# Expert outputs kept as rows in device memory and fetched by each token, for seven of eight experts

## The chip, the cores and the metric

The kernel runs on one core of one Trainium2 chip. The metric is the device time of one execution in microseconds (us); three runs of the kernel before give 1876.14 us as their median.

## The reference, cut to what matters

Two layers of a hybrid decoder trunk (four mixer groups, cross attention, a feed-forward part) on 256 tokens of 1024 numbers, all in float32. The second layer ends with eight SwiGLU experts, of which each token uses two:

```python
def moe_swiglu(h, router, wg, wu, wd):
    logits = (h @ router).astype(jnp.float32)
    top_v, top_i = lax.top_k(logits, TOP_K)                 # TOP_K = 2
    gates = jax.nn.softmax(top_v, axis=-1)
    combine = jnp.sum(jax.nn.one_hot(top_i, N_EXPERTS, dtype=jnp.float32) * gates[..., None], axis=-2)
    out = jnp.zeros_like(h)
    for e in range(N_EXPERTS):                              # 8 experts, wg and wu 1024x3584, wd 3584x1024
        out = out + combine[..., e:e + 1].astype(h.dtype) * swiglu(h, wg[e], wu[e], wd[e])
    return out
```

## The kernel before

The first 880 us are the two layers up to the experts. The change touches only `experts()`, of which every engine has its own copy (ACT L858, DVE L1500, PE L2323), the block of GpSimd (L1738) and the loads of SP.

**Passes and steps.** An expert is one pass `p` of at most 128 tokens (an expert with more gets a second pass behind the eight; with these inputs none does). A pass has 7 steps `j` of 512 columns of the 3584, so there are 56 steps `s = 7p + j`. Each step uses six chunks of 1 MB of weights: four for gate and up, two for down. SP loads chunk `m` into one of six raw buffers (`ex_raw`, `XRAW = 6`: three of their own, two in `PT`, one in `TMP`) as soon as DVE has read chunk `m - 6` there. ACT copies a chunk to a rounded "hi" (L863), DVE subtracts to get a "lo" (L1023, `x_chunk`), both into one of four pairs of buffers (`XSPL = 4`), which come free when PE has used chunk `m - 4`. PE makes each product in three passes (hi by hi, lo by hi, hi by lo).

**The order of PE** is written out by hand: `turn(s-1)` (four transposes, L2407), `gate_up(s)` (48 matmuls of 512 columns, L2371), `down(s-1)` (24 matmuls, L2381), so the down product of a step comes one step late and hides the activation on ACT and DVE (`prod`, `act_hi`, `act_lo`).

**Tokens to slots.** `one_hots` (DVE, L1551) writes a matrix `oneh` of tokens by slots. `turn_slots(p)` (PE) turns it with two transposes (L2448) and, for `p > 0`, makes the list of token rows with four small matmuls (L2451, two in the source, each as two in the trace). DVE's `turned(p)` takes both out: `slot_index` (L1564) and the turned one-hot `onehT` (L1565). GpSimd fetches the 128 token rows of a pass from `token_rows` in device memory into `picked` with an indirect DMA (L1750), and PE turns them (`gather`, L2462).

**Slots back to tokens.** When pass `q` is done, ACT copies its output to `yE` hi (`expert_output`, L892), DVE makes `yE` lo (`output_lo`, L1558), PE multiplies both with `onehT` (`scatter(q, hf)`, L2480: four matmuls of 512 columns per half, eight per expert), and DVE adds the result, times the gate, into the residual `x` (`scattered`, L1579, four per expert). For the first seven experts the two halves of `scatter` stand before and after `down` in step 1 of the next pass; for the last one they stand at the end.

**Gates and tables.** At `s == 2` DVE runs `gates_and_passes` between the lo of chunk 13 and `act_lo(1)`: 15 small operations in a row. Chunks 14 and 15 are those of `down(1)`.

Of the kernel before, what the change touches and what calls it, by code (L numbers as in the profile page):

```python
# [14 lines left out]
P = 128  # L15
D = 1024
# [93 lines left out]
def build(nc, A, out):  # L110
# [14 lines left out]
    with ExitStack() as ctx:  # L125
# [30 lines left out]
        onehT_flat = shared("onehT", 512, 4 * 1024 * (7 - 4), F32R)  # L156
# [182 lines left out]
        STORED = 16 * (TT + 2)  # L339
        SECONDS = TT * P * 2 // (P + 1)  # L340
        oneh = mt(3)[:, 0:256]
        onehT = [onehT_flat[:, 256 * i:256 * i + 256] for i in range(2)]
# [144 lines left out]
        def _(act):  # L487
# [370 lines left out]
            def experts():  # L858
# [22 lines left out]
                def expert_output(q):  # L881

                    if q == NE - 1:
                        act.wait_ge(S("tm_half"), 6)
                    else:
                        act.wait_ge(S("chunk_done"), n_straight + xd(q * XSTEPS + XSTEPS - 1, 1) + 1)
                    if q:
                        act.wait_ge(S("ex_sc"), 4 * q)
                    for hf in range(2):
                        if hf and q == NE - 1:  # L890
                            act.wait_ge(S("chunk_done"), n_straight + NX)
                        nc.scalar.activation(yE[0][:, 512 * hf:512 * hf + 512], ps[:, 4 + hf, :], ACT.Copy).then_inc(S("ex_yhi"), 1)  # L892
# [43 lines left out]
                added[0] = act.value_load(pass_count[0:1, 0:1], min_val=4 * NE - 1, max_val=4 * (NE + SECONDS) - 1)  # L936
# [60 lines left out]
        def _(dve):  # L997
# [502 lines left out]
            def experts():  # L1500
# [72 lines left out]

                def scattered(q, hf):

                    for t in range(TT):
                        dve.wait_ge(S("ex_sc"), q * 4 + (2 * hf + t + 1))
# [14 lines left out]
                turned(0)  # L1592
# [4 lines left out]
                def gates_and_passes():  # L1597

                    dve.wait_ge(S("rt_p"), 1)
                    for t in range(TT):  # L1600
                        ts(o[:, t, 0, :], o[:, t, 0, :], weight[:, t, 0:1], ALU.mult)
                        stt(gate[:, t, :], o[:, t, 1, :], weight[:, t, 1:2], o[:, t, 0, :], ALU.mult, ALU.add)
# [7 lines left out]
                    ts(col(ST_N1), col(ST_N1), 4.0, ALU.mult, float(4 * NE - 1), ALU.add)  # L1610
# [9 lines left out]
                for s in range(XS):  # L1620
# [17 lines left out]
                    if j == 1 and p:  # L1638
                        scattered(p - 1, 0)
# [4 lines left out]
                    if j == 1 and p:  # L1644
                        scattered(p - 1, 1)
# [14 lines left out]
                for hf in range(2):  # L1660
                    output_lo(hf, 2 * NE - 1 + hf)
                for hf in range(2):
                    scattered(NE - 1, hf)
                for o in range(SECONDS):
                    with dve.If(which[o] < NE):
# [11 lines left out]
                        dve.wait_ge(S("ex_gt"), o + (NE + 1))  # L1677
# [19 lines left out]
                        for hf in range(2):  # L1697
                            for t in range(TT):
                                dve.wait_ge(S("ex_sc"), o * 4 + (4 * NE + 2 * hf + t + 1))
# [38 lines left out]
        def _(pool):  # L1738
            G = nc.gpsimd
            pool.wait_ge(S("eps_xs"), 1 + TT)  # L1740
            for hf in range(2):
                pool.dma_start(token_rows[0:1, 512 * hf:512 * hf + 512], tmp(4)[0:1, :]).then_inc(S("ex_rows"), 16)
# [3 lines left out]
            for p in range(1, NE):  # L1746
                pool.wait_ge(S("ex_index"), p)
                if p > 1:
                    pool.wait_ge(S("ex_g"), 2 * p)
                G.indirect_dma_start(picked, None, token_rows, bass.IndirectOffsetOnAxis(slot_index, 0)).then_inc(S("ex_rows"), 16)  # L1750

        @block.tensor
        def _(pe):
# [569 lines left out]
            def experts():  # L2323
# [118 lines left out]
                def turn_slots(p):  # L2442

                    pe.wait_ge(S("ex_sel"), p * 2 + 2)
                    if p:
                        pe.wait_ge(S("ex_selT"), p)
                    for t in range(TT):
                        ins = pe.transpose(ps[:, 3, P * t:P * t + P], oneh[:, P * t:P * t + P], ident)  # L2448
                    if p:
                        for t in range(TT):  # L2450
                            ins = pe.matmul(ps[:, 3, 256:257], oneh[:, P * t:P * t + P], slot_row[t], start=t == 0, stop=t == 1)  # L2451
                    ins.then_inc(S("ex_gt"), 1)

                def gather(p):

                    if p > 1:
                        pe.wait_ge(S("ex_x"), 4 * (p - 1))
                    if p:
                        pe.wait_ge(S("ex_rows"), STORED + 16 * p)
# [10 lines left out]
                def scatter(q, hf):  # L2470

                    pe.wait_ge(S("ex_y"), q * 2 + (hf + 1))
                    if hf == 0:
                        pe.wait_ge(S("ex_selT"), q + 1)
                        pe.wait_ge(S("ex_hlo"), KT * min(q + 2, NE))
                    for t in range(TT):
                        if hf and q < NE - 1:
                            pe.wait_ge(S("ex_x"), q * 4 + (t + 1))
                        for i in range(2):
                            ins = pe.matmul(ps[:, out_bank(q, hf) + t, :], onehT[q % 2][:, P * t:P * t + P], yE[i][:, 512 * hf:512 * hf + 512],  # L2480
# [6 lines left out]
                turn_slots(0)  # L2487
                for s in range(XS):
# [20 lines left out]
                with pe.Fori(0, SECONDS) as o:  # L2509
                    which = pe.value_load(pass_expert[0:1, bass.ds(o + NE, 1)], min_val=0, max_val=NE)  # L2510
                    with pe.If(which < NE):
# [5 lines left out]
                        pe.wait_ge(S("ex_x"), 4 * NE)  # L2517
# [22 lines left out]
                        pe.wait_ge(S("ex_selT"), o + (NE + 1))  # L2540
                        for hf in range(2):
                            pe.wait_ge(S("ex_y"), o * 2 + (2 * NE + hf + 1))
                            for t in range(TT):
                                if hf:
                                    pe.wait_ge(S("ex_x"), o * 4 + (4 * NE + t + 1))
# [103 lines left out]
```

## Time and profile before

| | |
|---|---|
| median of 3 runs | 1876.14 us (1874.97 to 1878.23) |
| the profiled execution, its own time | 1873.28 us |
| its span, first to last instruction | 1871.4 us (1.9 us lie around it) |
| mean granted TensorE clock | 0.995 |
| busy over the span | PE 97%, weight loads 84%, DVE 76%, ACT 62%, GpSimd 9.1 us |
| moved by DMA | 470.75 MB, mean 252 GB/s; 363 to 395 GB/s while the experts run |

The chain of work that ended last is 92% PE. A busy PE does not mean PE at its peak, since matmuls overlap; what a matmul costs is read from the distance of its start to the next one's, not from its duration. Times in rows are microseconds from the start of the span, means of one are in nanoseconds.

### The profile page before, as it was taken

Reading aid. Unit: us, or ns where it says so; the run is one execution under the profiler, and the core shown is the slowest. Engines: PE = TensorE matmul, PEld = TensorE weight load, DVE = VectorE, ACT = ScalarE, POOL = GpSimd, SP = SyncE. Lnnn points to the kernel's source line nnn. Section 1 sums busy time; section 2 is a strip of 40 time slices with the busy share of each in tenths; the row PEclk is TensorE's granted clock in tenths of the full one; section 3 lists DMA queues with packets and bytes.
Section 4 is the critical chain, followed back from the end, with each engine's and each line's share of the span. In section 5 each row is a group of like instructions: output and inputs, shape, how many; then the busy total and the mean of one; then the engine's idle time right before and its main releaser. Section 6 shows DMA issues by size and latency. Waiting matters only on the chain.

```text
span 1871.4 us, 29948 instructions
## 1 busy us (share of the span) xinstructions
PE 1815.1 (97%) x12628; PEld 1565.2 (84%) x12629; DVE 1429.3 (76%) x1468; ACT 1154.5 (62%) x1127; POOL 9.1 (0%) x15
## 2 busy tenths in 40 slices
PE   7989999999999998999999999999999999999996
PEld 7977789999999977798888888888888888888885
DVE  7875654544458776554999999899998998989986
ACT  6565344443444655445777777777777777767774
POOL 0000000000000000000000000000000000000000
PEclk9999999999999999999999999999999999999998
DMA  8511224455636212235999999999999999999992
GB/s 254 180 59 58 70 91 173 140 191 188 203 127 208 94 48 69 91 136 196 332 380 383 363 366 374 375 374 363 356 381 370 369 368 363 379 371 363 368 374 114
DMA packets 240830, 470.75 MB, mean 252 GB/s; under 512 B 12080, under 2 KB 87984, under 8 KB 240688
## 3 DMA queue, kind: packets, MB, share of 16 engines
q1 hardware_dynamic: 239184, 463.93, 69.1%
q0 software_dynamic: 1360, 4.72, 0.6%
q8 instruction: 102, 1.67, 0.4%
q14 instruction: 40, 0.33, 0.1%
q10 hardware_dynamic: 144, 0.11, 0.0%
HBM read 466.62 MB, written 2.10 MB: 250 GB/s over the span
## 4 chain that ended last, share of the span: by engine, by line
PE 92%; DVE 5%; issue 1%; ACT 1%; DMA 0%; SPq 0%; DVEq 0%; ACTq 0%
PE ps L2371 32%; PE ps L1772 16%; PE ps L2381 16%; PE ps L1757 14%; PE ps L1794 8%; PE ps L2407 1%; PE ps L1839 1%; DVE MT L1003 1%; PE ps L2480 1%; PE ps L2362 1%; DVE MT L1006 0%; DVE TMP L1003 0%; DMA raw<-in_w_in 0%; DVE MT L1263 0%; PE ps L2462 0%
## 5 line engine op out<-in xcount | busy, mean ns | idle before, releaser
L1023 DVE TENSOR_TENSOR wlo<-raw,whi 128x2048 fp32r<-128x2048 f32 x140 | 320.6, 2290 | 42.7 <-ACT whi L863 42.6
L863 ACT ACTIVATE whi<-raw 128x2048 fp32r<-128x2048 f32 x140 | 269.1, 1922 | 128.3 <-PE ps L2381 71.3
L1016 DVE TENSOR_TENSOR wlo<-raw,whi 128x2048 fp32r<-128x2048 f32 x85 | 194.4, 2288 | 80.7 <-ACT whi L505 80.6
L505 ACT ACTIVATE whi<-raw 128x2048 fp32r<-128x2048 f32 x85 | 162.1, 1908 | 83.7 <-PE ps L1794 31.8
L1023 DVE TENSOR_TENSOR wlo<-PT,whi 128x2048 fp32r<-128x2048 f32 x84 | 192.1, 2291 | 28.1 <-ACT whi L863 28.0
L863 ACT ACTIVATE whi<-PT 128x2048 fp32r<-128x2048 f32 x84 | 161.4, 1922 | 35.2 <-PE ps L2371 34.6
L2371 PE MATMUL ps<-whi,hE_hi 128*128 128x512 f32 x660 | 182.1, 398 | 0.0
L2371 PE MATMUL ps<-wlo,hE_hi 128*128 128x512 f32 x660 | 177.0, 390 | 0.0
L2371 PE MATMUL ps<-whi,hE_lo 128*128 128x512 f32 x660 | 176.6, 389 | 0.0
L2371 PEld LDWEIGHTS ps<-wlo,hE_hi 128*128 128x128 f32 x660 | 123.9, 188 | 26.8
L2371 PEld LDWEIGHTS ps<-whi,hE_lo 128*128 128x128 f32 x660 | 123.9, 188 | 26.3
L2371 PEld LDWEIGHTS ps<-whi,hE_hi 128*128 128x128 f32 x660 | 119.8, 188 | 21.8
L2381 PE MATMUL ps<-whi,act_lo 128*128 128x512 f32 x332 | 129.3, 389 | 0.0
L2381 PE MATMUL ps<-whi,act_hi 128*128 128x512 f32 x332 | 129.1, 389 | 0.0
L2381 PE MATMUL ps<-wlo,act_hi 128*128 128x512 f32 x332 | 129.1, 389 | 0.0
L1772 PE MATMUL ps<-hT_hi,whi 128*128 128x256 f32 x848 | 120.8, 285 | 0.0
L1772 PE MATMUL ps<-hT_hi,wlo 128*128 128x256 f32 x848 | 119.0, 283 | 0.0
L1772 PE MATMUL ps<-hT_lo,whi 128*128 128x256 f32 x848 | 119.0, 283 | 0.0
L1772 PEld LDWEIGHTS ps<-hT_hi,whi 128*128 128x128 f32 x848 | 110.1, 192 | 2.3 <-issue 1.4
L496 ACT ACTIVATE MT<-ps 128x512 f32<-128x512 f32 (+2 forms) x96 | 45.1, 469 | 104.9 <-PE ps L1772 51.5
L1772 PEld LDWEIGHTS ps<-hT_lo,whi 128*128 128x128 f32 x848 | 109.4, 192 | 0.0
L1772 PEld LDWEIGHTS ps<-hT_hi,wlo 128*128 128x128 f32 x848 | 109.4, 192 | 0.0
(342 smaller groups left out, 3309.3 us busy)
## 6 DMA issues: line engine op xcount, KB each, us to landing
raw<-in_moe_w_up SPq DMA_DIRECT2D x111, 1024.0 KB, 7.1
PT<-in_moe_w_down SPq DMA_DIRECT2D x56, 1024.0 KB, 6.2
PT<-in_moe_w_gate SPq DMA_DIRECT2D x55, 1024.0 KB, 6.7
TMP<-in_moe_w_gate SPq DMA_DIRECT2D x55, 1024.0 KB, 6.7
raw<-in_moe_w_down SPq DMA_DIRECT2D x55, 1024.0 KB, 6.1
raw<-in_w_in SPq DMA_DIRECT2D x28, 1024.0 KB, 5.5
raw<-in_ffn_w_gate SPq DMA_DIRECT2D x11, 1024.0 KB, 5.3
raw<-in_ffn_w_up SPq DMA_DIRECT2D x11, 1024.0 KB, 5.4
```

The source lines that it names most:

```text
L496: return chain.link(lambda: nc.scalar.activation(o, i, f, **kw))
L505: nc.scalar.activation(whi[i % SPL][:, :], raw[d % RAW][:, :], ACT.Copy).then_inc(S("w_hi"), 1)
L863: nc.scalar.activation(ex_hi[m % XSPL], ex_raw[m % XRAW], ACT.Copy).then_inc(S("w_hi"), 1)
L1003: return chain.link(lambda: V.tensor_tensor(o, x0, x1, op))
L1016: V.tensor_tensor(wlo[i % SPL][:, :], raw[d % RAW][:, :], whi[i % SPL][:, :].bitcast(F32), ALU.subtract).then_inc(S("w_lo"), 1)
L1023: V.tensor_tensor(ex_lo[m % XSPL], ex_raw[m % XRAW], ex_hi[m % XSPL].bitcast(F32), ALU.subtract).then_inc(S("w_lo"), 1)
L1757: return Signalled(pe.matmul(o, lhsT, rhs, start=start, stop=stop, skip_group_check=True))
L1772: ins = pe.matmul(ps[:, bank, SEQ * m:SEQ * m + SEQ], wp[a_][:, k, P * m:P * m + P], src[b_][:, k, :], start=i == 0 and k == 0, stop=last)
L1794: ins = pe.matmul(ps[:, 4 + 2 * t + hf, :], src(b_, kk, t), wp[a_][:, kk, 512 * hf:512 * hf + 512], start=first and kk == 0 and i == 0, st ...
L1839: ins = pe.matmul(ps[:, bank, SEQ * m:SEQ * m + SEQ], wp[a_][:, k, P * m:P * m + P], hT[b_][:, k, :], start=p_ == 0 and k == 0 and m == 0, ...
L2371: ins = pe.matmul(ps[:, bank, :], h_[b_][:, X_K * i + k, :], wp[a_][:, k, :], start=i == 0 and n_ == 0 and k == 0, stop=i == 1 and n_ == 2 ...
L2381: ins = pe.matmul(ps[:, 4 + hf, :], act_[b_][:, P * (TM_ROWS * i + kk):P * (TM_ROWS * i + kk) + P], wp[a_][:, kk, 512 * hf:512 * hf + 512] ...
```

## The change

The outputs of experts 0 to 6 no longer go through `yE` lo, the one-hot product and four adds each. ACT copies the output of a pass to `mt(6)` in SBUF, and GpSimd stores it as 128 rows of a new tensor `output_rows` in device memory (512 KB). `gates_and_passes` also works out, for each token and each of its two choices, which row that is (row 0, which is zeros, for an output of expert 7 or of a second pass): eight more small operations. In the last pass, in steps 2 to 5, GpSimd fetches into `picked` the rows that the 128 tokens of a half take for their first or second choice (four indirect DMAs of 512 KB), and DVE adds each with its gate into `x` (`add_picked`, 128x1024). Expert 7 and second passes go as before. The one-hot is turned by PE for expert 7 alone. GpSimd waits for each store and each fetch to land before its next step. `down` of step 0 of a pass waits for ACT's copy, no longer for DVE's lo.

```diff
+        output_rows = nc.dram_tensor("output_rows", (P * (NE - 1) + 1, D), F32, kind="Internal").ap()
+        output_index = col(251, 2 * TT).bitcast(U32)
+        STORED = 16 * (TT + 4)
+        rows_stored = lambda q: STORED + 16 * (2 * q + 2)
+        rows_picked = lambda p: STORED + 16 * (2 * p - 1)
+        outputs_picked = lambda k: rows_stored(NE - 2) + 16 * (k + 1)
...
@@ ACT, expert_output(q)
                     if q:
-                        act.wait_ge(S("ex_sc"), 4 * q)
+                        act.wait_ge(S("ex_rows"), rows_stored(q - 1))
+                    to = yE[0][:, :] if q == NE - 1 else mt(6)
...
@@ DVE
                 def turned(p):
 
-                    dve.wait_ge(S("ex_gt"), p + 1)
-                    if p:
-                        V.tensor_copy(slot_index, ps[:, 3, 256:257]).then_inc(S("ex_index"), 1)
-                    V.tensor_copy(onehT[p % 2], ps[:, 3, 0:256]).then_inc(S("ex_selT"), 1)
+                    dve.wait_ge(S("ex_gt"), p)
+                    V.tensor_copy(slot_index, ps[:, 3, 256:257]).then_inc(S("ex_index"), 1)
+                    if p == NE - 1:
+                        V.tensor_copy(onehT[0], ps[:, 3, 0:256]).then_inc(S("ex_selT"), 1)
...
+                def add_picked(k):
+
+                    t = k // 2
+                    dve.wait_ge(S("ex_rows"), outputs_picked(k))
+                    if k:
+                        dve.wait_ge(S("ex_x"), k)
+                    V.scalar_tensor_tensor(out=x[:, t, :], in0=picked, scalar=col(ST_W + k), in1=x[:, t, :],
+                                           op0=ALU.mult, op1=ALU.add).then_inc(S("ex_x"), 1)
...
-                turned(0)
...
                     dve.wait_ge(S("rt_p"), 1)
+                    place, of, inside = (mt(5)[:, a_:a_ + 4].rearrange("p (t k) -> p t k", t=2) for a_ in (128, 132, 136))
+                    at = mt(5)[:, 160:192].rearrange("p (t k n) -> p t k n", t=2, k=2)
+                    tt(at, o, rank.unsqueeze(2).to_broadcast([P, 2, 2, 8]), ALU.mult)
+                    chain.link(lambda: V.tensor_reduce(place, at, AX, ALU.add))
+                    ts(inside, place, float(P), ALU.is_lt)
+                    ts(of, idf[:, :, 0:2], float(NE - 1), ALU.is_lt)
+                    tt(inside, inside, of, ALU.mult)
+                    stt(place, idf[:, :, 0:2], float(P), place, ALU.mult, ALU.add)
+                    stt(place, place, 1.0, inside, ALU.add, ALU.mult)
+                    chain.link(lambda: V.tensor_copy(output_index, mt(5)[:, 128:132]))
...
@@ DVE, loop over the steps
-                        if p and j == 1:
-                            for hf in range(2):
-                                output_lo(hf, 2 * p - 1 + hf)
...
-                    if j == 1 and p:
-                        scattered(p - 1, 0)
...
-                    if j == 1 and p:
-                        scattered(p - 1, 1)
...
+                    if 2 <= j < 2 + 2 * TT and p == NE - 1:
+                        add_picked(j - 2)
...
@@ GpSimd
                 G.indirect_dma_start(picked, None, token_rows, bass.IndirectOffsetOnAxis(slot_index, 0)).then_inc(S("ex_rows"), 16)
+                pool.wait_ge(S("ex_rows"), rows_picked(p))
+                pool.wait_ge(S("ex_yhi"), 2 * p)
+                at = 1 + P * (p - 1)
+                pool.dma_start(output_rows[at:at + P, :], mt(6)).then_inc(S("ex_rows"), 16)
+                pool.wait_ge(S("ex_rows"), rows_stored(p - 1))
+            pool.wait_ge(S("ex_table"), 1)
+            pool.wait_ge(S("ex_g"), 2 * NE)
+            for k in range(2 * TT):
+                if k:
+                    pool.wait_ge(S("ex_x"), k)
+                G.indirect_dma_start(picked, None, output_rows, bass.IndirectOffsetOnAxis(output_index[:, k:k + 1], 0)).then_inc(S("ex_rows"), 16)
...
@@ PE
                     if p and j == 0:
-                        pe.wait_ge(S("ex_y"), 2 * p)
+                        pe.wait_ge(S("ex_yhi"), 2 * p)
...
                 def turn_slots(p):
 
                     pe.wait_ge(S("ex_sel"), p * 2 + 2)
+                    if p > 1:
+                        pe.wait_ge(S("ex_index"), p - 1)
+                    if p == NE - 1:
+                        for t in range(TT):
+                            pe.transpose(ps[:, 3, P * t:P * t + P], oneh[:, P * t:P * t + P], ident)
+                    for t in range(TT):
+                        ins = pe.matmul(ps[:, 3, 256:257], oneh[:, P * t:P * t + P], slot_row[t], start=t == 0, stop=t == 1)
+                    ins.then_inc(S("ex_gt"), 1)
...
                 gather(0)
-                turn_slots(0)
...
-                    if p and j == 1:
-                        scatter(p - 1, 0)
                     if s:
                         down(s - 1)
-                    if p and j == 1:
-                        scatter(p - 1, 1)
```

What the cut leaves out are counts of semaphores that follow from this, two more stores of 2 KB for the row of zeros, and DVE's wait for the four adds before it adds expert 7.

## Rows read from the trace of the kernel before

**Rows 1.** The page, part 1: busy time, share, instructions.

```profile
PE 1815.1 (97%) x12628; PEld 1565.2 (84%) x12629; DVE 1429.3 (76%) x1468; ACT 1154.5 (62%) x1127; POOL 9.1 (0%) x15
```

**Rows 2.** By stretch: length, busy per engine (instructions), PE clock, DMA share, GB/s.

```profile
1000.00:1100.00 100.00, 100.00 (x461) 83.04 (x460) 90.75 (x65) 74.29 (x57) 0.96 (x1) 1.00 1.02 376
...
1700.00:1800.00 100.00, 100.00 (x455) 82.80 (x454) 92.19 (x62) 74.97 (x50) 0.00 (x0) 1.00 1.00 368
```

**Rows 3.** Who waited for whom, 850 to 1820 us: total, times, longest.

```profile
ACT whi L863 <- DMA raw<-in_moe_w_gate: 3.8, 1, 3.8
...
PEld ps L2407 <- DVE MT L1540: 1.3, 1, 1.3
```

**Rows 4.** The same for the DMA queue of SP: total, times, longest.

```profile
SPq L466 <- DVE wlo L1023: 632.3, 245, 17.5
```

**Rows 5.** Chain that ended last, experts 0 to 2: start, length, what.

```profile
1021.22 10.93 PE ps L2371 x48
1032.15 0.91 PE ps L2480 x4
...
1038.50 0.91 PE ps L2480 x4
...
1039.85 10.91 PE ps L2371 x48
...
1056.20 0.22 PE ps L2448 x2
...
1160.77 10.91 PE ps L2371 x48
```

**Rows 6.** The same chain where the first expert starts.

```profile
889.51 0.22 PE ps L2448 x2
...
929.86 5.44 PE ps L2381 x24
```

**Rows 7.** Instructions of DVE in order of time: start, length, line, tiles.

```profile
922.77 0.22 DVE L1006 TENSOR_SCALAR MT<-MT,st 128x8 f32<-128x8 f32 x1
...
926.03 0.69 DVE L1544 TENSOR_TENSOR act_lo<-ps,act_hi 128x512 fp32r<-128x512 f32 x1
926.64 2.28 DVE L1023 TENSOR_TENSOR wlo<-raw,whi 128x2048 fp32r<-128x2048 f32 x1
```

**Rows 8.** By stretch of 20 us, columns as in rows 2: the fullest ones.

```profile
940.00:960.00 20.00, 20.00 (x96) 16.70 (x95) 17.50 (x13) 14.00 (x10) 1.00 (x1) 1.00 1.04 391
960.00:980.00 20.00, 20.00 (x91) 16.54 (x90) 18.36 (x18) 17.18 (x19) 0.00 (x0) 1.00 1.04 389
...
1360.00:1380.00 20.00, 20.00 (x92) 16.56 (x91) 17.64 (x11) 14.88 (x10) 0.00 (x0) 1.00 1.04 395
```

**Rows 9.** Tile raw, 1000 to 1500 us: loads from issue to landing.

```profile
DMA to landing us min/median/max: 4.7/6.9/8.4
```

**Rows 10.** Line 1750, GpSimd's fetch of token rows: durations, and issue to landing.

```profile
L1750 POOL DMA_INDIRECT TMP<-token_rows,st x7: 936/937/998, 941.4 to 1665.5; - x7
...
DMA to landing us min/median/max: 6.2/6.9/7.6
```

**Rows 11.** DMA issues: tiles, queue, count, KB each, us to landing.

```profile
token_rows<-PT POOLq DMA_DIRECT2D x2, 512.0 KB, 3.4
```

**Rows 12.** Groups by line and shape, 780 to 1872 us: busy, mean ns.

```profile
L1579 DVE SCALAR_TENSOR_TENSOR x<-ps,st,x 128x512 f32<-128x512 f32 x32 | 22.4, 743 | 0.0
...
L1558 DVE TENSOR_TENSOR yE_lo<-ps,yE_hi 128x512 fp32r<-128x512 f32 x16 | 10.3, 681 | 5.0 <-ACT yE_hi L892 5.0
...
L1009 DVE SCALAR_TENSOR_TENSOR x<-x,st,PT 128x1024 f32<-128x1024 f32 x2 | 2.6, 1284 | 0.1
```

**Rows 13.** Issues of SP in order of time: a load into TMP.

```profile
1037.92 0.37 SPq L466 DMA_DIRECT2D TMP<-in_moe_w_gate  x1
```

**Rows 14.** Instructions of ACT in order of time: copy of an output; that chunk is read.

```profile
1022.71 1.06 ACT L892 ACTIVATE yE_hi<-ps 128x512 fp32r<-128x512 f32 x2
...
1050.85 1.92 ACT L863 ACTIVATE hT_hi<-TMP 128x2048 fp32r<-128x2048 f32 x1 [0.80 <-PE ps L2371]
```

More of the change, by code:

```diff
@@ L155, in build @@
         yE = [shared(f"yE_{s}", 1024, 4 * 1024 * (7 - i), F32R) for s, i in (("hi", 2), ("lo", 5))]
-        onehT_flat = shared("onehT", 512, 4 * 1024 * (7 - 4), F32R)
+        onehT_flat = shared("onehT", 256, 4 * 1024 * (7 - 4), F32R)
         TMP = sb("TMP", 8 * 512)
@@ L336, in build @@
         token_rows = nc.dram_tensor("token_rows", (SEQ + 1, D), F32, kind="Internal").ap()
+        output_rows = nc.dram_tensor("output_rows", (P * (NE - 1) + 1, D), F32, kind="Internal").ap()
         picked = TMP[:, 2048:2048 + D]
         slot_row, slot_index = [col(248 + t) for t in range(TT)], col(250).bitcast(U32)
-        STORED = 16 * (TT + 2)
+        output_index = col(251, 2 * TT).bitcast(U32)
[3 more added lines that the diff above has]
+        outputs_picked = lambda k: rows_stored(NE - 2) + 16 * (k + 1)
+        ADDED = 2 * TT + 4
         SECONDS = TT * P * 2 // (P + 1)
         oneh = mt(3)[:, 0:256]
-        onehT = [onehT_flat[:, 256 * i:256 * i + 256] for i in range(2)]
+        onehT = [onehT_flat[:, 0:256]]
         def ff_chunk(j):
@@ L891, in expert_output @@
                             act.wait_ge(S("chunk_done"), n_straight + NX)
-                        nc.scalar.activation(yE[0][:, 512 * hf:512 * hf + 512], ps[:, 4 + hf, :], ACT.Copy).then_inc(S("ex_yhi"), 1)
+                        nc.scalar.activation(to[:, 512 * hf:512 * hf + 512], ps[:, 4 + hf, :], ACT.Copy).then_inc(S("ex_yhi"), 1)
                 chain.settle()
@@ L935, in experts @@
                 which = [act.value_load(pass_expert[0:1, NE + o:NE + o + 1], min_val=0, max_val=NE) for o in range(SECONDS)]
-                added[0] = act.value_load(pass_count[0:1, 0:1], min_val=4 * NE - 1, max_val=4 * (NE + SECONDS) - 1)
+                added[0] = act.value_load(pass_count[0:1, 0:1], min_val=ADDED - 1, max_val=ADDED + 4 * SECONDS - 1)
                 expert_output(NE - 1)
@@ L1609, in gates_and_passes @@
                     chain.link(lambda: V.tensor_reduce(col(ST_N1), col(ST_OVER, NE), AX, ALU.add))
-                    ts(col(ST_N1), col(ST_N1), 4.0, ALU.mult, float(4 * NE - 1), ALU.add)
+                    ts(col(ST_N1), col(ST_N1), 4.0, ALU.mult, float(ADDED - 1), ALU.add)
                     chain.link(lambda: V.tensor_copy(pass_count, col(ST_N1)))
@@ L1661, in experts @@
                     output_lo(hf, 2 * NE - 1 + hf)
+                dve.wait_ge(S("ex_x"), 2 * TT)
                 for hf in range(2):
@@ L1676, in experts @@
                         dve.wait_ge(S("ex_sel"), o * 2 + (2 * NE + 2))
-                        dve.wait_ge(S("ex_gt"), o + (NE + 1))
+                        dve.wait_ge(S("ex_gt"), o + NE)
                         V.tensor_copy(onehT[0], ps[:, 3, 0:256]).then_inc(S("ex_selT"), 1)
@@ L1741, in _ @@
             for hf in range(2):
-                pool.dma_start(token_rows[0:1, 512 * hf:512 * hf + 512], tmp(4)[0:1, :]).then_inc(S("ex_rows"), 16)
+                for rows in (token_rows, output_rows):
+                    pool.dma_start(rows[0:1, 512 * hf:512 * hf + 512], tmp(4)[0:1, :]).then_inc(S("ex_rows"), 16)
             for t in range(TT):
@@ L2444, in turn_slots @@
                     pe.wait_ge(S("ex_sel"), p * 2 + 2)
-                    if p:
-                        pe.wait_ge(S("ex_selT"), p)
+                    if p > 1:
[3 more added lines that the diff above has]
+                            pe.transpose(ps[:, 3, P * t:P * t + P], oneh[:, P * t:P * t + P], ident)
                     for t in range(TT):
[L2448 to L2451, printed above, removed]
+                        ins = pe.matmul(ps[:, 3, 256:257], oneh[:, P * t:P * t + P], slot_row[t], start=t == 0, stop=t == 1)
                     ins.then_inc(S("ex_gt"), 1)
                 def gather(p):
-                    if p > 1:
-                        pe.wait_ge(S("ex_x"), 4 * (p - 1))
                     if p:
-                        pe.wait_ge(S("ex_rows"), STORED + 16 * p)
+                        pe.wait_ge(S("ex_rows"), rows_picked(p))
                     for c in range(KT):
@@ L2470, in scatter @@
                 def scatter(q, hf):
-                    pe.wait_ge(S("ex_y"), q * 2 + (hf + 1))
+                    pe.wait_ge(S("ex_y"), hf + 1)
                     if hf == 0:
-                        pe.wait_ge(S("ex_selT"), q + 1)
-                        pe.wait_ge(S("ex_hlo"), KT * min(q + 2, NE))
+                        pe.wait_ge(S("ex_selT"), 1)
+                        pe.wait_ge(S("ex_hlo"), KT * NE)
                     for t in range(TT):
-                        if hf and q < NE - 1:
-                            pe.wait_ge(S("ex_x"), q * 4 + (t + 1))
                         for i in range(2):
-                            ins = pe.matmul(ps[:, out_bank(q, hf) + t, :], onehT[q % 2][:, P * t:P * t + P], yE[i][:, 512 * hf:512 * hf + 512],
+                            ins = pe.matmul(ps[:, out_bank(q, hf) + t, :], onehT[0][:, P * t:P * t + P], yE[i][:, 512 * hf:512 * hf + 512],
                                             start=i == 0, stop=i == 1)
@@ L2516, in experts @@
                         ins.then_inc(S("ex_gt"), 1)
-                        pe.wait_ge(S("ex_x"), 4 * NE)
+                        pe.wait_ge(S("ex_x"), ADDED)
                         for c in range(KT):
```

10 lines of the change are left out of this document (5 added, 5 removed).

## Prediction

> **What bounds the kernel now.** I read the page's busy line first [rows 1]: PE is busy for 97% of the span, DVE for 76%. An average over stages does not say what an edit in one stage is worth, so next come the stretches of 100 us while the experts run [rows 2]. There are eight such stretches from 1000 to 1800 us, all alike: PE 100.00 of 100.00 at full clock, DVE 90 to 92, ACT 73 to 76, and the DMA engines at a share of 0.98 to 1.02. Two resources look full, PE and DMA, and the whole forecast hangs on which of them is the limit. The list of waits decides it [rows 3, 4]. From 850 to 1820 us ACT, the first reader of a chunk, waited for a load once, for 3.8 us; the only wait of PE's loads inside the steps is one of 1.3 us at the first turn. SP waited 632.3 us in 245 waits (more for the other buffers) for DVE to free a raw buffer. A DMA queue that waits for free buffers, and readers that do not wait for data, mean that loads are on time. The third view is the chain that ended last [rows 5]: from 902 to 1849 us it is PE without a gap, so a matmul taken away there shortens the kernel, as long as the loads, the split into hi and lo, and the new waits keep up.
>
> **What leaves PE.** In the chain each half of a scatter takes 0.91 us, between a gate_up of 10.93 us and the down [rows 5]. Two halves for each of seven experts: 7 x 2 x 0.91 = 12.74 us. Turning the one-hot takes 0.22 us for two transposes [rows 5]. It goes in six of the seven turns that lie inside the steps (the one for expert 7 stays), and once more ahead of the first gate_up, where it stands in the chain too [rows 6]: 7 x 0.22 = 1.54 us. All of it is on the path: 14.28 us. The pitch of an expert is now 1160.77 - 1039.85 = 120.92 us [rows 5]; it becomes 118.88 us.
>
> **What leaves DVE and what comes.** Per expert two `output_lo` at 0.681 us and four adds at 0.743 us go [rows 12], 4.33 us, and the copy of the turned one-hot with them. That is off the path, for DVE has some 9 us of each 100 free [rows 2], but it means that DVE cannot become the limit of experts 1 to 6. In the last pass four `add_picked` come. The nearest row is the same operation on 128x1024 with all operands in SBUF, 1.284 us [rows 12]: 5.1 us, against the 4.33 us that leave that pass, and spread over four steps. I cost them at nothing; cover is DVE's free time, some 1.5 us of a step of 16.8 us.
>
> **Eight small operations at s = 2.** Here DVE is not ahead. It runs without a gap, catching up from the start of the experts. The 15 small operations of `gates_and_passes` take from 922.77 to 926.03 us, 0.217 us each [rows 7]. The first lo that `down(1)` needs (chunk 14) is then made from 926.64 to 928.92 us [rows 7], and `down(1)` starts at 929.86 us [rows 6]. The slack is 0.94 us. Eight more operations are 8 x 0.217 = 1.74 us, a little more for the one over 32 columns: 1.8 us. So PE will wait 1.8 - 0.94 = 0.9 us once, at the first `down` behind them. Chunk 15 is needed 2.7 us after chunk 14 and is made in 2.2 us, so it does not add a second wait. Bounds: zero, if the small operations cost under 0.12 us each, and 1.8 us, if the slack is an artefact of how the trace models ends. I take 0.9 us.
>
> **GpSimd and the new waits.** GpSimd's own order is now fetch, wait, store, wait. Behind its wait for ACT's copy of pass p - 1 (step 0 of pass p) stands only the fetch for pass p + 1, whose index comes in step 3, some 50 us later. A plain store of 512 KB landed in 3.4 us when the queues were half empty [rows 11]; under load I bound it by the slowest load of 1 MB, 8.4 us [rows 9]. Either ends long before step 3: cost zero. DVE waits for each of the four fetches, with the lo of the next chunks behind it, and PE behind those. A fetch of the same size takes 0.94 us on GpSimd and 6.9 us to land, 7.6 us at worst [rows 10]. The first can start some 15 us after pass 6 ends and is asked for more than 30 us after that end; the others have a step, 16.8 us, each. Cost zero; the cover is 16.8 - 7.6 - 0.94 - 1.3 = 7 us per step. `down` of step 0 waits for ACT's copy: it ends at 1023.77 us [rows 14], 8.4 us ahead of where that `down` would start (1032.15 us [rows 5]). ACT's wait for the last store has a whole pass.
>
> **The transfers.** This is the part that can go wrong. A pass loads 42 chunks of 1.049 MB, 44.04 MB, and fetches 0.52 MB: 44.56 MB in 120.92 us, 368.5 GB/s. Afterwards it is 45.09 MB (the store is added) in 118.88 us: 379 GB/s. In steps 2 to 5 of the last pass it is 6.29 + 0.52 MB in 16.8 us, 405 GB/s. What can the engines do? The fullest stretches of 20 us show 391, 389 and 395 GB/s at a share of 1.04 [rows 8], the first two of them side by side and with a fetch in them. I take 390. Then experts 1 to 6 fit with 3% to spare. In the last pass each fetch costs 1.34 us of the engines where a step leaves 0.69 us free; over four fetches and the last store that is a backlog of 5 x 0.65 = 3.3 us. The ring of raw buffers can take it: a load into TMP issued at 1037.92 us is first read at 1050.85 us [rows 13, 14], 12.9 us later, and a load lands in 6.9 us [rows 9], so 6.0 us are to spare before ACT waits, and PE has about 3 us more behind ACT and DVE. So: zero.
>
> **A rule that speaks against this.** The Trainium skill, page "DMA: Bandwidth & Descriptors", section "Where 436 GB/s comes from", says that for transfers between HBM and SBUF the HBM side binds, at about 358 GB/s per core. By that rule the stream here would be at its limit already and the bytes added would be paid in full, which is the slower rival below. The trace disagrees with the figure: it shows 376 GB/s over 100 us and 395 over 20 [rows 2, 8]. The page "SBUF — State Buffer" (section "The single rule") warns that VectorE and GpSimd lock each other out of a shared port, which would hit a kernel with GpSimd stores beside a busy VectorE. The rows do not show it: each fetch holds GpSimd for 936 to 998 ns while VectorE is 90% busy [rows 2, 10].
>
> **The sum.** 12.74 + 1.54 - 0.9 = 13.4 us. Against the profiled execution: its own time of 1873.28 us (span 1871.4) gives 1859.9 us. The median of the runs is 2.9 us above the profiled one, and I carry that over: 1876.14 - 13.4 = 1862.7 us.
>
> **Rivals.**
> - *A backlog in the last pass.* If the engines give only 379 GB/s when stores and fetches are mixed in, the five extra transfers leave 5 x 1.1 = 5.6 us of backlog and experts 1 to 6 run with no reserve, so the ring drains. PE would wait some 2 to 6 us: 1865 to 1869 us. For it: the share is already 1.0. Against it: the stretches at 390.
> - *DMA takes over as the limit; slower.* The change adds 7 x 0.524 + 4 x 0.524 = 5.77 MB. If the present mean of 370 GB/s were all that there is, then PE would gain nothing from doing less, and the bytes would cost 5.77 / 0.370 = 15.6 us: up to 1876.1 + 15.6 = 1892 us. It decides from 45.09 MB / 120.92 us = 373 GB/s downwards: above that a pass is no longer than now. Against it stand ACT's missing waits for loads [rows 3] and rows 8.
> - *A fetch is late.* If fetches of output rows take over 14 us (rows 10 say 7.6 at most), each makes DVE late; PE notices when that exceeds 3 us more, so at 20 us per fetch it costs about 3 us each: 1863 + 12 = 1875 us.
> - *The products leave but their time does not.* Had the scatters filled a time in which PE must wait anyway, nothing would move: 1876 us. Steps without a scatter run back to back as well [rows 5], which is against it.
>
> **How the numbers follow.** The forecast gets 0.76, the backlog 0.11, DMA as the limit 0.06, the late fetch 0.04, no effect 0.03. The forecast's own range is the stall at zero or 1.8 us, the runs' scatter of about 1 to 2 us and a little more: 1859 to 1866. The backlog case takes the top to 1869. Measurement of this kernel can tell 0.2%, 3.8 us. Faster by more than that: 0.76 + 0.11 and a part of the late fetches, 0.88. Within: 0.06. Slower: DMA as the limit, 0.06.
>
> **What the profile would show.** Right: L2480 with 8 matmuls instead of 64, the pitch of an expert 118.9 us and PE still without gaps; a wait of PE before `down(1)` of about 0.9 us; 90% DMA share or more with 375 to 382 GB/s in the stretches of 100 us; SP still waiting for DVE. Wrong: waits of ACT for raw buffers (DMA the limit), landings of loads over 12 us, waits of DVE for `ex_rows` before the adds, or a second wait of PE behind the small operations. The prediction would be wrong first of all if the mean rate cannot rise from 370 to 379 GB/s.

## The result and the profile after

The changed kernel takes 1865.79 us (median of 5 runs, 1864.32 to 1868.32), the kernel before 1876.14 us. The difference of the medians is 10.4 us. The ratio is 0.9949 with a 95% interval of 0.9937 to 0.9960, which is 9.6 us, between 7.5 and 11.8. Forecast were 13.4 us and 1862.7 us. The measured median lies at the upper edge of the forecast's own range (1859 to 1866); 1869 was the end of the backlog case.

The span of the profiled execution went from 1871.4 to 1862.4 us. The busy line of the page answers to [rows 1], and two of the stretches of 100 us to [rows 2] (length, busy per engine, clock, DMA share, GB/s):

```profile
PE 1804.2 (97%) x12558; PEld 1555.2 (84%) x12559; DVE 1408.0 (76%) x1431; ACT 1154.2 (62%) x1127; POOL 23.7 (1%) x28
```

```profile
1000.00:1100.00 100.00, 100.00 (x461) 83.03 (x460) 88.31 (x57) 75.26 (x58) 1.53 (x2) 1.00 1.03 389
1700.00:1800.00 100.00, 100.00 (x454) 82.79 (x453) 90.93 (x51) 75.48 (x50) 5.06 (x4) 1.00 1.04 392
```

PE is as full as before, and the DMA engines now carry 376 to 392 GB/s in the eight stretches of 100 us from 1000 to 1800 us (364 to 376 before). PE did not have to wait for them: the list of waits from 850 to 1820 us has the same single wait of ACT for a load as [rows 3], and two waits of PE that are new.

```profile
ACT whi L869 <- DMA raw<-in_moe_w_gate: 4.0, 1, 4.0
...
PE ps L2493 <- DMA TMP<-token_rows,st: 1.3, 1, 1.3
...
PE ps L2414 <- DVE wlo L1030: 0.9, 1, 0.9
```

L2414 is `down`, L2493 is the turning of fetched token rows (`gather`). Both waits lie in the first pass. The chain that ended last shows where (start, length, what); it answers to [rows 5, 6]:

```profile
904.16 10.92 PE ps L2404 x48
...
945.09 11.76 DMA TMP<-token_rows,st
956.84 0.04 issue
956.89 1.09 PE ps L2493 x8
...
1077.32 10.91 PE ps L2404 x48
...
1196.19 10.92 PE ps L2404 x48
...
1823.11 10.91 PE ps L2404 x48
```

Gate and up of step 11 start at 1077.32 us and those of step 18 at 1196.19 us, a pitch of 118.87 us per expert where 120.92 us stood before [rows 5] and 118.88 us was forecast.

The most useful measure of this case is the distance from the second `gate_up` to the last. It holds the whole work on the experts and neither the stretch ahead of them nor the end. Before it is 1832.56 - 902.15 = 930.41 us, after 1823.11 - 904.16 = 918.95 us: 11.46 us less. The other parts of the span went the wrong way in these two profiles: 2.01 us more ahead of the second `gate_up`, and 0.45 us more behind the start of the last one. 11.46 - 2.01 - 0.45 = 9.0 us, the difference of the spans.

So three things were to be explained: a fetch that landed after 11.8 us, the wait at `down`, and 2 us ahead of the experts, in a part of the program that the change hardly touches.

### The profile page after: what moved, and what is told of

The parts are those of the page before. It is cut to its first block, busy times and chain, and to the rows that moved or that the text cites. A ratio compares the mean times of both kernels' runs of the same rounds, so it can differ in the third digit from the quotient of the medians.

```text
span 1862.4 us, 29775 instructions
## 1 busy us (share of the span) xinstructions
PE 1804.2 (97%) x12558; PEld 1555.2 (84%) x12559; DVE 1408.0 (76%) x1431; ACT 1154.2 (62%) x1127; POOL 23.7 (1%) x28
## 4 chain that ended last, share of the span: by engine, by line
PE 90%; DVE 7%; issue 1%; DMA 1%; ACT 1%; DVEq 0%; SPq 0%; ACTq 0%; POOLq 0%
PE ps L2404 31%; PE ps L1805 16%; PE ps L2414 15%; PE ps L1790 15%; PE ps L1827 8%; PE ps L2440 1%; PE ps L1872 1%; DVE MT L1010 1%; DVE wlo L1030 1%; DMA TMP<-token_rows,st 1%; PE ps L2395 1%; DVE MT L1013 0%; DMA raw<-in_w_in 0%; DVE TMP L1010 0%; DVE hT_lo L1030 0%
## 5 line engine op out<-in xcount | busy, mean ns | idle before, releaser
L2404 PEld LDWEIGHTS ps<-wlo,hE_hi 128*128 128x128 f32 x660 | 123.9, 188 | 26.8
L2414 PE MATMUL ps<-whi,act_hi 128*128 128x512 f32 x332 | 129.2, 389 | 0.9 <-DVE wlo L1030 0.9
L2414 PE MATMUL ps<-whi,act_lo 128*128 128x512 f32 x332 | 129.3, 389 | 0.0
L2414 PE MATMUL ps<-wlo,act_hi 128*128 128x512 f32 x332 | 129.2, 389 | 0.0
```

What stands on the lines that cost most here:

```text
L2404: ins = pe.matmul(ps[:, bank, :], h_[b_][:, X_K * i + k, :], wp[a_][:, k, :], start=i == 0 and n_ == 0 and k == 0, stop=i == 1 and n_ == 2 ...
L2414: ins = pe.matmul(ps[:, 4 + hf, :], act_[b_][:, P * (TM_ROWS * i + kk):P * (TM_ROWS * i + kk) + P], wp[a_][:, kk, 512 * hf:512 * hf + 512] ...
```

## The experiments

### The changed kernel again, and the kernel before twice

No edit.

> The changed kernel once more, beside the others on one chip. The loss against the forecast (3 us) has three candidates: (A) in the stretch before the experts the granted TensorE clock falls to half for 3.4 us at 140 and at 230 us, which cost 2 us in the profile of after and is chance; (B) PE waits about 1.1 us at the first down behind the eight small operations; (C) PE waits 1.3 us for the first fetch of token rows, which held GpSimd for 5.05 us. If A is chance, the time from the start of the span to the first expert changes by up to 2 us from profile to profile; if A belongs to the kernel, every profile of it shows both dips. B and C should come back at the same size: 0.87 and 1.25 us of idle PE.

> The kernel before, for a second profile. In the first one GpSimd's first fetch began at 941.43 us, 0.02 us ahead of the next operation of DVE with two SBUF inputs (941.45 us); if that is luck, a second profile may show it shut out for 2 to 5 us. If the dips of the clock before the experts are chance, the second gate_up starts at 902 us (two dips up to then) or 1.7 us later per further dip; if they belong to the changed kernel, always at 902 us. From the last gate_up to the end: 38.8 us as before, if the 0.5 us more of the changed kernels belongs to them.

> A third profile of the kernel before, for the same three questions: length of the first fetch (1.0 us, or 2 to 5 us when DVE comes first), start of the second gate_up (902 us, or later by 1.7 us per dip of the clock), and time from the last gate_up to the end (38.8 us).

Measured: e1_again 1865.27 us, ratio 0.9945 (0.9932 to 0.9959). The starts of the second and the last `gate_up`, from the chains of after (shown above), e1_again and the two runs of before:

```profile
904.91 10.92 PE ps L2404 x48
1823.84 10.92 PE ps L2404 x48
```

```profile
903.17 10.92 PE ps L2371 x48
1833.62 10.91 PE ps L2371 x48
```

```profile
907.19 10.91 PE ps L2371 x48
1837.59 10.91 PE ps L2371 x48
```

The distance is 918.93 us for the changed kernel and 930.45 and 930.40 us for the one before. It repeats within 0.05 us, so a tenth of a microsecond can be read from one profile, which the timed medians (2 us of scatter) do not allow. Both waits of PE came back in e1_again, at 0.9 and 1.2 us. The time ahead of the second `gate_up` does not repeat: 902.15, 903.17 and 907.19 us in the same kernel before. What differs there is the granted clock. In these stretches, of before and of after in turn, the clock is the third number from the end:

```profile
130.00:150.00 20.00, 15.90 (x232) 13.21 (x232) 17.69 (x30) 8.32 (x14) 0.00 (x0) 1.00 0.19 56
225.00:245.00 20.00, 18.81 (x169) 15.81 (x169) 9.51 (x13) 5.12 (x8) 0.00 (x0) 1.00 0.30 106
```

```profile
130.00:150.00 20.00, 17.36 (x232) 14.32 (x232) 17.79 (x30) 8.13 (x14) 0.00 (x0) 0.91 0.19 56
225.00:245.00 20.00, 18.82 (x148) 15.77 (x146) 9.52 (x13) 5.29 (x9) 0.00 (x0) 0.91 0.31 106
```

A dip from 2.4 to 1.2 GHz, one in each stretch, in code that is the same in both kernels. The second and third profile of before have such a dip in the first of these stretches too, and the third has one more near 760 us and is the slowest of before. The changed kernel with four stores (below) had neither and started at 902.72 us. Over all profiles of changed kernels the second `gate_up` starts between 902.72 and 905.16 us, inside the spread of the three of before (902.15 to 907.19). So the 2 us are chance (candidate A in the expectation) and no part of the change, as far as 13 profiles can tell.

The first fetch of the kernel before held GpSimd for 1.00 us in all three profiles, though it began only 0.02 to 0.03 us ahead of the operation of DVE. The end, from the last `gate_up` on, took 38.84, 38.78 and 38.71 us before and 39.3 to 39.6 us in the changed kernels (it was not read for the one with eight stores).

### Two copies on DVE behind the first index

```diff
                     V.tensor_copy(slot_index, ps[:, 3, 256:257]).then_inc(S("ex_index"), 1)
+                    if p == 1:
+                        for k in range(2):
+                            V.tensor_copy(mt(4)[:, 256 + 256 * k:512 + 256 * k], ps[:, 3, 0:256])
```

> After, with two copies of 128x256 out of PSUM (0.33 us of DVE each) behind the copy of the first slot_index, where the removed copy of the turned one-hot stood. Port theory: a fetch by index is shut out while DVE runs operations with two SBUF inputs back to back, and the removed copy had given GpSimd the gap; then the first fetch holds GpSimd for 1.0 us again, lands in about 7 us, PE does not wait for it, and the kernel is 1.3 to 1.5 us faster than e1_again. Rival (code or descriptor start-up of GpSimd, or full queues): the first fetch takes 5 us as before and nothing is gained.

Measured: 1863.90 us, ratio 0.9941 (0.9928 to 0.9955). The first fetch on GpSimd, in after and in e2 (start, length):

```profile
945.09 5.05 POOL L1772 DMA_INDIRECT TMP<-token_rows,st  x1 [59.41 <-DVE st L1570]
```

```profile
945.52 1.00 POOL L1775 DMA_INDIRECT TMP<-token_rows,st  x1 [59.37 <-DVE st L1570]
```

It landed after 7.7 us, and PE no longer waits for it. The distance is 1822.09 - 904.60 = 917.49 us, 1.46 us less than after. Adding work to DVE made the kernel faster by this measure; the medians of e2 and e1_again differ by 1.37 us, which their intervals do not tell apart. The instructions of DVE in after show how:

```profile
944.11 0.15 DVE L1570 CAST st<-ps 128x1 uint32<-128x1 f32 x1
944.18 0.68 DVE L1551 TENSOR_TENSOR act_lo<-ps,act_hi 128x512 fp32r<-128x512 f32 x1
944.78 2.28 DVE L1030 TENSOR_TENSOR wlo<-raw,whi 128x2048 fp32r<-128x2048 f32 x1
946.97 2.29 DVE L1030 TENSOR_TENSOR wlo<-PT,whi 128x2048 fp32r<-128x2048 f32 x1
949.53 2.29 DVE L1030 TENSOR_TENSOR wlo<-PT,whi 128x2048 fp32r<-128x2048 f32 x1 [0.26 <-ACT whi L869]
```

The index is there at 944.26 us and GpSimd begins at 945.09. By then DVE runs an operation that reads two tiles in SBUF, and another behind it without a gap. DVE's first gap begins at 949.26 us; GpSimd's fetch ends at 950.14, 0.88 us after that, a little less than the 0.94 to 1.00 us that an undisturbed one takes. In the kernel before the same copy of the index was followed by the copy of the turned one-hot:

```profile
941.43 1.00 POOL L1750 DMA_INDIRECT TMP<-token_rows,st  x1 [58.63 <-DVE st L1564]
...
940.45 0.15 DVE L1564 CAST st<-ps 128x1 uint32<-128x1 f32 x1
940.52 0.41 DVE L1565 CAST onehT<-ps 128x256 fp32r<-128x256 f32 x1
940.85 0.68 DVE L1544 TENSOR_TENSOR act_lo<-ps,act_hi 128x512 fp32r<-128x512 f32 x1
941.45 2.30 DVE L1023 TENSOR_TENSOR wlo<-raw,whi 128x2048 fp32r<-128x2048 f32 x1
```

There GpSimd began at 941.43 us and came first. The change took away 0.33 us of DVE's time and with it GpSimd's head start. The rival, a start-up of code or descriptors, would not have gone away with two copies on DVE. The lengths repeat: 5.04 to 5.05 us in all five profiles that have the small operations in step 2 and no copies (after, e1_again and the last three experiments below), 1.00 us in e2 and in the two later kernels with the copies.

### The eight new operations later

```diff
+                def places_of_outputs():
...
+                    if s == 9:
+                        places_of_outputs()
...
-                        ts(o[:, t, 0, :], o[:, t, 0, :], weight[:, t, 0:1], ALU.mult)
+                        ts(first, o[:, t, 0, :], weight[:, t, 0:1], ALU.mult)
```

`places_of_outputs` holds the eight operations out of `gates_and_passes`; `first` is a scratch tile, so that the one-hots stay as they are.

> After, with the eight new small operations moved from step 2 to step 9, where DVE has time. If they cause the wait at down(1), it is gone (1.1 us), and DVE is early enough at the first fetch for its gaps to be back: the fetch then starts 2 us earlier against PE and its wait is zero too, 2.4 us faster than e1_again in all. If the wait at down(1) has another cause (a late load, ACT), it stays.

> e3 once more, since it is the best version: the distance from the second gate_up to the last again 916.3 us, no wait of PE between them, and a ratio to the kernel before of 0.993 to 0.994 (12 to 13 us).

Measured: 1862.92 us, ratio 0.9934 (0.9920 to 0.9947), and in the second run 1862.47 us, ratio 0.9931 (0.9917 to 0.9944). The two starts in e3:

```profile
905.16 10.91 PE ps L2411 x48
1821.50 10.91 PE ps L2411 x48
```

916.34 us in both runs (1821.29 - 904.95 in e11), and no wait of PE in between. This beats both kernels, by 2.6 us of distance against after; on one chip with e1_again it is 2.35 us by the medians. The wait at `down` was caused by the eight operations. Its price is what e2 keeps over e3: 917.49 - 916.34 = 1.15 us. The fetch of e3 was still shut out, but through one operation only. It landed 9.7 us after its start, ahead of where PE asks for it:

```profile
944.43 2.85 POOL L1779 DMA_INDIRECT TMP<-token_rows,st  x1 [58.35 <-DVE st L1570]
```

### All small operations later, and the copies

```diff
-                    if s == 2:
+                    if s == 9:
                         gates_and_passes()
```

and the two copies of e2.

> After, with all 23 small operations (old and new) in step 9 and the two copies behind the first slot_index. No wait of PE in the first pass is left: 2.4 to 2.8 us faster than e1_again, as e3 or a little more, since nothing else waits for DVE there. If clock dips before the experts outweigh this, the timed difference will be blurred by 1 us either way; the pitch of the starts of gate_up then decides. Against the kernel before: 13 us, ratio 0.993.

Measured: 1864.32 us, ratio 0.9943 (0.9929 to 0.9956), distance 919.12 us. No gain at all, against an expectation of 2.6 us. The first pass has no wait left, but now the second fetch was hit:

```profile
942.59 1.00 POOL L1775 DMA_INDIRECT TMP<-token_rows,st  x1 [56.87 <-DVE st L1570]
...
1063.95 5.08 POOL L1775 DMA_INDIRECT TMP<-token_rows,st  x1 [37.23 <-issue]
```

PE waited 0.9 us at a `down` and 1.4 us for that fetch, in the second pass. The 23 operations take some 5 us of DVE in step 9, so DVE runs without gaps in step 10, when the second index comes, as it did in the first pass of after. The expectation missed this, but it is a strong sign for the cause: the long fetch moves with DVE's backlog.

### The same in step 12

```diff
-                    if s == 9:
+                    if s == 12:
                         gates_and_passes()
```

> After, with all 23 small operations in step 12 (two steps behind the second slot_index, not one ahead of it as in e4) and the two copies behind the first slot_index. In e4 the second fetch held GpSimd for 5.08 us, because the operations had made DVE late in step 9. Port theory: with DVE on time at both turns, every fetch of token rows holds GpSimd for 1 us, PE has no gap from the second gate_up to the last, and the distance of their starts is 916.3 us (918.9 in after and e1, 919.1 in e4): 2.6 us faster than e1_again. Rival (the length of the fetch is chance or start-up): some fetch takes 5 us again.

Measured: 1868.11 us, ratio 0.9950 (0.9937 to 0.9964): 8.5 us faster than its own runs of the kernel before, where e3 was 12.5 us faster than its own. Half of the expectation held: all seven fetches of token rows took 0.97 to 1.00 us. The other half did not. DVE makes the lo of the next pass's tokens right ahead of step 12 (2.15 us for eight operations of L1581), and the small ones came on top, so PE waited 2.91 us at `down`, and then this happened (columns as above, stretches around the wait):

```profile
1090.00:1100.00 10.00, 10.00 (x48) 8.26 (x47) 8.87 (x22) 9.19 (x14) 0.00 (x0) 1.00 1.05 389
1100.00:1105.00 5.00, 2.82 (x13) 2.00 (x11) 4.55 (x15) 3.93 (x3) 0.00 (x0) 1.00 0.06 22
1105.00:1112.00 7.00, 6.27 (x15) 4.95 (x16) 7.00 (x5) 0.71 (x1) 0.00 (x0) 0.51 0.72 264
```

After the wait the granted clock was at its lower level for 7 us. The distance is 1826.91 - 904.55 = 922.36 us, 6.02 us above e3: 2.91 us of waiting and 3.1 us behind it, most of it the slow clock. The shorter waits of after (0.87 and 1.25 us) left the clock at 1.00. The choice of step 12 was my mistake: I had looked at the distance to the next index, and not at what else DVE does in that step.

### Without the rows

Stores, fetches of output rows and adds are taken out, and with them the outputs of seven experts. ACT's copies and the eight small operations stay; ACT's wait for the last store becomes one for DVE's `hE_lo`.

```diff
-                at = 1 + P * (p - 1)
-                pool.dma_start(output_rows[at:at + P, :], mt(6)).then_inc(S("ex_rows"), 16)
-                pool.wait_ge(S("ex_rows"), rows_stored(p - 1))
...
-                G.indirect_dma_start(picked, None, output_rows, bass.IndirectOffsetOnAxis(output_index[:, k:k + 1], 0)).then_inc(S("ex_rows"), 16)
...
-                        add_picked(j - 2)
```

> After without the seven stores, the four fetches of output rows and the four adds (so the outputs of experts 0 to 6 are left out of the result). If these transfers cost nothing, as forecast, the distance from the second gate_up to the last stays 918.9 us and the time that of after, 1865 to 1866 us. If the DMA engines were the limit, 5.8 MB less would give back up to 15 us.

Measured: 1864.59 us (4 runs), ratio 0.9934 (0.9919 to 0.9950); distance 1823.60 - 904.71 = 918.89 us, 0.06 us less than after. By the distance, seven stores, four fetches and four adds of 1.28 us cost nothing; the medians agree within their intervals. Its first fetch took 5.05 us as well, so the stores are not what delays it.

### Four and eight stores of each output

```diff
                 pool.dma_start(output_rows[at:at + P, :], mt(6)).then_inc(S("ex_rows"), 16)
+                for k in range(3):
+                    pool.dma_start(spare_rows[P * k:P * k + P, :], mt(6)).then_inc(S("ex_rows"), 16)
```

(7 instead of 3 in the second; counts of `ex_rows` to match.)

> After, with each output stored four times (three of them into spare rows): 46.7 MB per pass in 118.9 us is 392 GB/s. By my capacity of 390 GB/s this stands right at the limit: 0 to 5 us slower over all. If the engines were full at 370 GB/s, 7 x 1.57 MB would cost 30 us.

> After, with each output stored eight times: 48.8 MB per pass. At 390 GB/s a pass takes 125 us in place of 118.9: some 35 us slower over all, with waits of ACT for raw buffers. At 370 GB/s it would be near 70 us; if there is room to 410, zero.

Measured, one run each: 1863.12 us and 1892.59 us. With four stores the distance is 1821.74 - 902.72 = 919.02 us, 0.07 us more than after, at this rate and with short waits of ACT for loads (5.0 us in four, 1.8 us the longest) that do not reach PE:

```profile
1400.00:1500.00 100.00, 100.00 (x460) 83.07 (x460) 89.46 (x57) 74.87 (x55) 0.98 (x1) 1.00 1.04 392
```

With eight the limit is there, and it looks quite different: the same stretch, and ACT's costliest wait for loads in the list of waits (total, times, longest), where after has a single one of 4.0 us.

```profile
1400.00:1500.00 100.00, 96.94 (x442) 79.14 (x441) 85.19 (x57) 71.70 (x53) 2.89 (x1) 1.00 1.04 398
```

```profile
ACT whi L870 <- DMA raw<-in_moe_w_up: 85.0, 51, 5.3
```

Its fetches of token rows start 122.9, 123.3 and 122.7 us apart in the second to fifth pass, so a pass takes 123 us: 48.8 MB in 123 us is 397 GB/s. That is what the engines can carry in this mix. After needs 379. The kernel is 26.8 us slower than after; 35 us were expected, for a capacity of 390.

This run also tests the head start within one kernel. From the second pass on, too, DVE has the next `wlo` to make right behind `act_lo`. The fetches of the second to sixth pass begin about 0.25 us into such a `wlo`, an operation with two inputs in SBUF, and take 2.89 to 2.90 us. In the seventh, where `turned` still copies the one-hot behind the index, the fetch begins 0.08 us ahead of the `wlo` and takes 0.99 us:

```profile
1067.16 2.89 POOL L1773 DMA_INDIRECT TMP<-token_rows,st  x1 [34.56 <-issue]
...
1682.09 0.99 POOL L1773 DMA_INDIRECT TMP<-token_rows,st  x1 [36.95 <-issue]
```

## Why the prediction was right, and where it was off

- **PE as the limit**: right. In after PE has no gap from the second pass to the last, and its work is what moved the time.
- **What leaves PE**: 12.74 us for the scatters, right to the last digit: with 0.22 us for each of six turns the distance should be 930.41 - 12.74 - 1.32 = 916.35 us, and e3, where nothing waits, has 916.34.
- **The seventh turn**, ahead of the first `gate_up` [rows 6], seems to have given nothing: from the writing of the first one-hots to the second `gate_up` it is 18.45 us before (883.70 to 902.15) and 18.46 after (885.70 to 904.16). But a dip of the clock lies over the transposes of `gather(0)` in every profile, and not at the same place. Over their first 4 us the granted clock was 0.64 in before, where the 32 transposes took 5.18 us, and 0.59 in after, where they took 5.39:

```profile
884.33 5.18 PE ps L2465 x32
```

```profile
886.33 5.39 PE ps L2496 x32
```

  The second profile of before had 0.59 too, and there the stretch is 18.64 us, against 18.46 in after and 18.43 in e2, also at 0.59. At the same clock the turn gave its 0.2 us, so the term of 1.54 us holds, and the 0.01 us of the first comparison is chance.
- **Eight operations at s = 2**: 0.94 us of slack less 1.8 us of work, 0.9 us forecast; PE's wait is 0.87 us in the list, 1.15 us by the distance. The term was right to 0.25 us. Of the 0.28 us between the two readings, 0.08 are the first matmul behind the wait (932.73 to 933.04 us from its start to the next one's, where 0.23 us is usual); the rest is open.
- **The fetch of token rows**: this step failed. I priced fetches at 0.94 us on GpSimd and 6.9 us to land, from seven equal rows [rows 10], and called the copy of the one-hot that leaves DVE a thing off the path. It landed after 11.8 us and cost 1.46 us (e2). The rule of the Trainium skill, page "SBUF — State Buffer", section "Who interferes with whom", on the port that VectorE and GpSimd share was before me, and I dismissed it with rows that could not test it. In the first fetch GpSimd had come first, by 0.02 us. The other six met no operation of DVE with two inputs in SBUF at all, as the second one shows: `act_lo` reads PSUM and SBUF, and the next `wlo` starts 0.22 us after the fetch has left GpSimd.

```profile
1060.88 0.96 POOL L1750 DMA_INDIRECT TMP<-token_rows,st  x1 [118.45 <-DVE st L1564]
```

```profile
1060.85 0.68 DVE L1544 TENSOR_TENSOR act_lo<-ps,act_hi 128x512 fp32r<-128x512 f32 x1
1062.06 2.29 DVE L1023 TENSOR_TENSOR wlo<-raw,whi 128x2048 fp32r<-128x2048 f32 x1 [0.53 <-ACT whi L863]
```

  A DVE that is 90% busy says nothing about what it runs when the fetch comes, and rows that agree with one another do not test a rule about who comes first.
- **The transfers**: costs of zero were right (e6), the rate of 379 GB/s held, and the capacity of 390 GB/s [rows 8] was low by 2% (e8: 397). Both DMA rivals fell: the one on the slower side would have needed less than 373. The late fetch of output rows fell too (they landed in 7.0 to 8.8 us), and so did the case that nothing moves. The Trainium skill, page "DMA: Bandwidth & Descriptors", section "Where 436 GB/s comes from", says that the HBM side binds at 358 GB/s per core, and gets this as 716 GB/s halved between two cores. With one core running, the trace went past it: 392 GB/s over 100 us. Read as the share of each of two busy cores it speaks neither for the slower rival nor against it; no run here had two.
- **The sum**: 13.4 us forecast, of which 0.2 us (the seventh turn) lies ahead of the second `gate_up`. Within the distance 13.16 us were forecast; 1.46 us of the fetch and 0.25 us more at `down` bring that to 11.45 us, and 11.46 were measured. The end costs another 0.5 us, so 11.2 us in all. The timed medians say 10.4 and 10.1 us (e1_again), which the interval does not tell from 11.2. Both misses and the end went the same way; that the median still fell inside the forecast's own range is owed to its margin, which was made for another reason (the stall at `down` and the scatter).
- **Open**: the 0.5 us at the end. In the chain of after the last stretch before the final norm runs through DVE's branches behind its adds, in before through ACT's. Nothing was tried on it, but e6 narrows it down: without the fetches of output rows and without their adds its end is 39.40 us, so these are not the cause.

## What to carry to other kernels

Removing an operation can cost time where it was a head start for another engine: for every edit on one engine ask who is released by the instruction just ahead, and what it will then meet. Price a small edit in its own step, not by the engine's free time over a stage; two placements of the same 23 operations gave nothing (step 9) and a wait and a slow clock (step 12, 3.4 us slower than after by the distance), while eight of them moved to step 9 gave 2.6 us. And measure between two landmarks of the engine that is the limit: that distance repeated within 0.05 us where whole runs scattered by 2 us.

## What the runs showed of the hardware

- A fetch by index on GpSimd is shut out while VectorE runs operations with two inputs in SBUF, until VectorE's next gap: 5.05 us in place of 1.00 through two such operations back to back, 2.85 us through one (e3), and 2.61 us for the first fetch of output rows in after, which began 0.54 us into one. In e1_again and e11 that last fetch began 0.56 and 0.47 us before the end of such an operation and took 1.42 and 1.33 us. In all of these it ended 0.86 to 0.88 us after VectorE's operation. An operation with one of its two inputs in PSUM did not hold it up: in after L1547 ran from 1751.58 to 1752.26 us, and the fetch of 2.61 us ended at 1752.52, 0.86 us after the `wlo` ahead of it.
- A plain store is not shut out. It took 0.56 us in the middle of such an operation:

```profile
1028.72 0.56 POOL L1776 DMA_DIRECT2D output_rows<-MT  x1 [78.59 <-ACT MT L899]
```

```profile
1027.23 2.29 DVE L1030 TENSOR_TENSOR wlo<-raw,whi 128x2048 fp32r<-128x2048 f32 x1 [0.43 <-ACT whi L869]
```

- The page "SBUF — State Buffer" of the Trainium skill, section "Who interferes with whom", says that a VectorE instruction with two SBUF inputs contends with a GpSimd instruction that reads SBUF, and not with one that only writes it. The trace agrees, if the fetch counts as the one that reads (its indices lie in SBUF) and the store as the one that does not.
- VectorE paid almost nothing when GpSimd came first: by 0.02 us in before, where its operation took 2.30 us in place of 2.29, and by 0.35 us in e2, where it started at 945.87 us, in the middle of the fetch, and took 2.28 us.
- TensorE kept 2.4 GHz through waits of 0.87 and 1.25 us inside a dense stretch. In e5 it was idle for 2.91 us, and the granted clock was at the lower level from 1105.0 us, 0.7 us ahead of its next matmul, to 1111.8 us. In the kernel with eight stores it was idle for 0.98 us and, some 3 us later, for 2.38 us; the clock was still 1.00 when it started again at 1788.90 us, and at the lower level from 1790.4 to 1793.9 us.
- The 16 DMA engines carried 397 to 398 GB/s of loads mixed with stores, at a busy share of 1.04. A share of 1.0 at 370 GB/s was therefore not the limit. The share does not tell the two apart: with four stores it was 1.04 as well, at 392 GB/s, and PE did not wait. ACT's waits for loads do.
